# A two-block transformer on one core: the modulation vector of the second block by row products on VectorE in place of accumulated rows and one-column products on TensorE

## The reference, cut to what matters

```
cond = jax.nn.silu(c)                                   # 1 x 1024
mod = (cond @ w_ada[layer] + b_ada[layer])[:, None, :]  # 1 x 6144
sh1, sc1, g1, sh2, sc2, g2 = jnp.split(mod, 6, axis=-1)
h = rms_norm_2(x, norm1_w[layer]) * (1.0 + sc1) + sh1
...
x = x + g1 * mix
h = rms_norm_2(x, norm2_w[layer]) * (1.0 + sc2) + sh2
...
x = x + g2 * ffn
```

## Time and profile before

| | |
|---|---|
| median of 3 runs | 2187.24 us (2186.93 to 2187.7) |
| profiled execution, own time | 2188.19 us |
| its span, first to last instruction | 2186.4 us |
| TensorE busy | 2131.9 us, 98% of the span |
| VectorE, ScalarE, GpSimd busy | 1037.7, 750.0, 890.1 us |
| mean granted TensorE clock | 0.987 |

### The profile page before, as it was taken

The page is one execution under the profiler, slowest core; times in us unless marked ns, Lnnn a source line. Parts: engine busy times, 40 slices in busy tenths (PEclk is TensorE's granted clock), DMA queues, the critical chain, the costliest instruction groups (busy, mean ns, idle before and its releaser), DMA issues.

```text
span 2186.4 us, 26047 instructions
## 1 busy us (share of the span) xinstructions
PE 2131.9 (98%) x9964; PEld 1685.0 (77%) x9964; DVE 1037.7 (47%) x1726; ACT 750.0 (34%) x1106; POOL 890.1 (41%) x717
## 2 busy tenths in 40 slices
PE   7999999999999999999999989999999998999999
PEld 5888888888888445888888867767778876888887
DVE  5445653562434895566256162655655644110111
ACT  4124321222223786322122243543454333222221
POOL 4445545454433211554455334222221243454444
PEclk9999999999999999999999989999999999999999
DMA  4223333422531000342442222111111122223222
GB/s 167 96 97 135 137 118 133 171 101 73 194 115 63 1 1 20 135 153 101 156 148 101 74 92 86 41 56 58 39 58 58 57 79 77 96 77 109 103 75 99
DMA packets 34204, 204.97 MB, mean 94 GB/s; under 512 B 4160, under 2 KB 5312, under 8 KB 14784
## 3 DMA queue, kind: packets, MB, share of 16 engines
q1 hardware_dynamic: 31968, 196.84, 25.6%
q10 hardware_dynamic: 2144, 6.88, 1.0%
HBM read 199.58 MB, written 2.10 MB: 92 GB/s over the span
## 4 chain that ended last, share of the span: by engine, by line
PE 68%; issue 14%; POOL 11%; DVE 4%; ACT 1%; DMA 0%; SPq 0%; POOLq 0%; DVEq 0%; ACTq 0%
PE PS L508 14%; PE PS L509 14%; PE PS L510 14%; POOL WL L446 11%; PE PS L599 4%; PE PS L601 3%; PE PS L600 3%; PE PS L777 2%; PE PS L790 2%; PE PS L808 2%; PE PS L958 1%; PE PS L926 1%; PE PS L920 1%; PE PS L1031 1%; PE PS L899 1%
## 5 line engine op out<-in xcount | busy, mean ns | idle before, releaser
L446 POOL TENSOR_TENSOR WL<-WR,WH 128x512 fp32r<-128x512 f32 (+2 forms) x692 | 858.5, 1271 | 1186.9 <-ACT WH L1152 1186.9
L508 PE MATMUL PS<-Hh,WH 128*128 128x512 f32 x1536 | 606.2, 395 | 22.9 <-DVE Hl L1679 9.8
L509 PE MATMUL PS<-Hl,WH 128*128 128x512 f32 x1536 | 601.3, 391 | 0.0
L510 PE MATMUL PS<-Hh,WL 128*128 128x512 f32 x1536 | 600.9, 391 | 0.0
L1152 ACT ACTIVATE WH<-WR 128x2048 fp32r<-128x2048 f32 (+2 forms) x173 | 305.9, 1768 | 702.3 <-PE PS L510 661.5
L508 PEld LDWEIGHTS PS<-Hh,WH 128*128 128x128 f32 x1536 | 290.6, 189 | 89.2 <-issue 14.6
L509 PEld LDWEIGHTS PS<-Hl,WH 128*128 128x128 f32 x1536 | 290.7, 189 | 62.2 <-issue 2.2
L510 PEld LDWEIGHTS PS<-Hh,WL 128*128 128x128 f32 x1536 | 290.5, 189 | 61.0
L508 PE MATMUL PS<-Gh,WH 128*128 128x512 f32 x592 | 232.2, 392 | 0.0
L509 PE MATMUL PS<-Gl,WH 128*128 128x512 f32 x592 | 232.0, 392 | 0.0
L510 PE MATMUL PS<-Gh,WL 128*128 128x512 f32 x592 | 231.7, 391 | 0.0
(11 more groups left out here) (279 smaller groups left out, 2372.6 us busy)
## 6 DMA issues: line engine op xcount, KB each, us to landing
WR<-wA SPq DMA_DIRECT2D x125, 1024.0 KB, 4.8
AW<-wada SPq DMA_DIRECT2D x24, 1024.0 KB, 6.8
WR<-wB SPq DMA_DIRECT2D x24, 768.0 KB, 4.1
WR<-wC SPq DMA_DIRECT2D x24, 640.0 KB, 3.9
X<-x_in SPq DMA_DIRECT2D x8, 256.0 KB, 6.5
W1K<-w1k ACTq DMA_DIRECT2D x1, 2048.0 KB, 8.0
W1V<-w1v ACTq DMA_DIRECT2D x1, 2048.0 KB, 12.9
out<-X SPq DMA_DIRECT2D x8, 256.0 KB, 4.8
```

The lines of the kernel that those rows point to most:

```text
L446: ins = nc.gpsimd.tensor_tensor(WL[:, s, piece], WR[:, s, piece], WH[:, s, piece].bitcast(F32), ALU.subtract)
L508: nc.tensor.matmul(PS[:, b, :], wh[:, c, cols], pe_h, start=c == 0, stop=False)
L509: nc.tensor.matmul(PS[:, b, :], wh[:, c, cols], pe_l, start=False, stop=False)
L510: last = nc.tensor.matmul(PS[:, b, :], wl[:, c, cols], pe_h, start=False, stop=c == seg.chunks - 1)
```

## The change

`modulation_unit` no longer accumulates rows with the inputs in the partitions. `w_ada` is stored transposed, so that a unit holds 2 x 128 outputs in the partitions and all 1024 inputs of each in the free dimension. Silu(c) is needed as one row that is the same in all partitions (CROW, 128x1024). A unit is then two `tensor_tensor_reduce` instructions of 128x1024 (product with CROW into a scratch AWC, sum into one column of MOD). `mod_sums` on TensorE goes away, and the bias is added to MOD in place.

The conditioning row comes by one DMA of 512 KB from `consts`, once at the start of each of the two FFNs (unit 1 of `gu0a` and `gu1a`, ahead of that unit's `load_ada`), and ScalarE applies Silu to it after the first body of that segment (`after_first=cond_row`). The old CSIL activation and its 8 parameter columns go away.

```diff
@@ sync: segment_with_ada
                     load_unit(seg, u % seg.upb, u // seg.upb)
+                    if u == units[0] and first % 12 == 0:
+                        sp.dma_start(CROW[:, :], consts[:, C_COND:C_COND + D]).then_inc(crow_s, 16)
                     if u in units:
                         a = first + units.index(u)
                         load_ada(a, a % 2)
@@ tensor: feed_forward
-                    if r == 1:
-                        mod_sums(l)
                     down(f"dn{l}{half}", g_ready)
-            def mod_sums(l):
-                pe.wait_ge(ada_acc_s, 12 * (l + 1))
-                if l:
-                    pe.wait_ge(mod_done, 1)
-                for n in range(24):
-                    mm = nc.tensor.matmul(PS[:, 5, n:n + 1], AACC[:, n * P:n * P + P], ones[:, 0:1],
-                                          start=True, stop=True)
-                mm.then_inc(mod_sum, 1)
@@ scalar: feed_forward
+                def cond_row():
+                    act.wait_ge(crow_s, 16 * l + 16)
+                    nc.scalar.activation(CROW[:, :], CROW[:, :], ACT.Silu).then_inc(cs_s, 1)
+
-                    dense(f"gu{l}{half}", evac)
+                    dense(f"gu{l}{half}", evac, after_first=cond_row if half == "a" and l < 2 else None)
@@ scalar: start
             act.wait_ge(par_s, 16)
-            nc.scalar.activation(CSIL[:, :], pcol("cond", 0, 8), ACT.Silu).then_inc(cs_s, 1)
@@ vector: feed_forward
                     if last:
-                        dve.wait_ge(mod_sum, l + 1)
-                        nc.vector.tensor_tensor(MOD[:, 24 * l:24 * l + 24], PS[:, 5, 0:24],
+                        chain.wait()
+                        dve.wait_ge(ada_acc_s, 12 * l + 12)
+                        nc.vector.tensor_tensor(MOD[:, 24 * l:24 * l + 24], MOD[:, 24 * l:24 * l + 24],
                                                 pcol("bada", 24 * l, 24), ALU.add).then_inc(mod_done, 1)
@@ vector: modulation_unit
-                acc = AACC[:, DS(256 * f, 256)]
-                for c in range(DC):
-                    w = AW[:, slot, c * 256:c * 256 + 256]
-                    if c == 0:
-                        chain.mark(nc.vector.tensor_scalar(acc, w, CSIL[:, 0:1], None, ALU.mult))
-                        chain.wait()
-                    elif c < DC - 1:
-                        chain.mark(nc.vector.scalar_tensor_tensor(acc, w, CSIL[:, c:c + 1], acc, ALU.mult, ALU.add))
-                        chain.wait()
+                if f == 0:
+                    dve.wait_ge(cs_s, n // 12 + 1)
+                chain.wait()
+                if n:
+                    dve.wait_ge(ada_acc_s, n)
+                for b in range(2):
+                    ins = nc.vector.tensor_tensor_reduce(
+                        out=AWC[:, b, :], in0=AW[:, slot, b * D:b * D + D], in1=CROW[:, :], scale=1.0, scalar=0.0,
+                        op0=ALU.mult, op1=ALU.add, accum_out=MOD[:, 2 * n + b:2 * n + b + 1])
+                    if b:
+                        ins.then_inc(ada_acc_s, 1)
                     else:
-                        nc.vector.scalar_tensor_tensor(acc, w, CSIL[:, c:c + 1], acc, ALU.mult, ALU.add)\
-                            .then_inc(ada_acc_s, 1)
+                        chain.mark(ins)
@@ host
-        "wada": units(tiles(a["w_ada_2"][0]), 2),
+        "wada": a["w_ada_2"][0].T.reshape(24, 2, P, D).transpose(0, 2, 1, 3).reshape(24, P, 2 * D),
+    c[:, C_COND:C_COND + D] = a["c_2"][0][None, :]
```

More of the change, by code:

```diff
@@ L87 @@
           ("norm1", 8), ("norm2", 8), ("conv1", 24), ("conv2", 48), ("conv2b", 12), ("ssdn", 8),
-          ("dskip", 8), ("qn", 1), ("kn", 1), ("bada", 48), ("cond", 8), ("pek", 16), ("pev", 16),
+          ("dskip", 8), ("qn", 1), ("kn", 1), ("bada", 48), ("pek", 16), ("pev", 16),
           ("dtb", 16), ("alog", 16), ("gatew", 384), ("dtw", 128), ("w2k", 256), ("w2v", 128)]
@@ L105 @@
 C_NONES = C_NTRI + P
-C_END = C_NONES + P
+C_COND = C_NONES + P
+C_END = C_COND + D
 def tile_of(k):
@@ L191, in two_blocks @@
         EPSC = at("EPSC", 205.75, [P, 3])
-        CSIL = at("CSIL", 205.8125, [P, DC])
         MOD = at("MOD", 205.5, [P, 48])
@@ L210, in two_blocks @@
         AW = at("AW", 166, [P, 2, KMAX])
-        AACC = at("AACC", 182, [P, 24 * P])
+        CROW = at("CROW", 182, [P, D])
+        AWC = at("AWC", 186, [P, 2, D])
         KV = at("KV", 48, [P, 12, T])
@@ L309, in two_blocks @@
         ada_s = [sem("ada0_loaded"), sem("ada1_loaded")]
-        mod_sum, mod_done = sem("mod_sums"), sem("mod_done")
+        mod_done, crow_s = sem("mod_done"), sem("cond_row_loaded")
         eps_s, cs_s = sem("eps_ready"), sem("cond_ready")
@@ L1828, in _ @@
             residual("wout", next_h=(Hh, Hl, "f_norm0"))
-            dve.wait_ge(cs_s, 1)
             feed_forward(0, next_h=(Hh, Hl, "b_norm"))
@@ L2364 @@
         "qn": cols(np.concatenate([a["q_norm_w_2"][0]] * 2)), "kn": cols(np.concatenate([a["k_norm_w_2"][0]] * 2)),
-        "bada": cols(a["b_ada_2"][0]), "cond": cols(a["c_2"][0]),
+        "bada": cols(a["b_ada_2"][0]),
         "pek": cols(a["cmp_pe_k"].reshape(-1)), "pev": cols(a["cmp_pe_v"].reshape(-1)),
```

## The result

The changed kernel takes 2176.95 us (median of five runs, 2176.39 to 2178.42) beside 2187.24 us for the kernel before (median of five runs made beside it). The ratio is 0.9939 with a 95% interval of 0.9927 to 0.9951. So it is faster, as forecast, but by 10.3 us where 15.8 were forecast, and 5.5 us above the predicted 2171.5. The profiled execution took 2178.21 us, of which 2.9 lie outside its span, between 2.5 and 2.9 in all five; in the kernel before it was 1.8. So about 1 us of what is missing is not in any span, and no trace shows what it is.

A forecast was written before the change was run, and what follows sets the result against it. TensorE's own instructions were taken to bound the kernel: 2188.19 - 15.77 for the columns, all other terms 0, gave 2172.4 us, or 2171.5 since the profiled execution was 0.95 above the median; range 2167.5 to 2177.

The forecast's parts named there:

- What bounds the kernel: First FFN's modulation stretch: TensorE's own instructions are the time, 300.00 of 300.00 us busy; work taken from it is gained fully.
- The columns, 15.77 us: Between up and down segments, two places: removing one-column matmuls gains 7.07 and 8.70 us, including 4.4 us of lowered clock behind.
- Rival (a): At the two places only the columns' own 11.55 us go, the clock falls anyway: 2175.7 us, chance 0.10.
- Does a wait take the freed place? Cost 0: At the down segment's start, gate rows and first two down units' weights, needed 5 to 6 us earlier, cause no wait.
- Rival (c): Nothing moves: a new wait eats the freed place, or columns ran under another engine's cover; 2187 us, chance 0.03.
- the clock elsewhere: Clock falls outside the two places, as in attention and mixer: 2.5 us down in the forecast's own range.
- rival (d): More is gained: clock falls in attention and mixer may come out shorter, or as well longer; 2167 us, chance 0.06.
- The products, 1.22 to 1.3 us: VectorE's modulation units: each 1024-element product takes 1.22 us, 1.3 with read-out, upper bound 2.44; a unit 3.9 us.
- GpSimd beside it, 5.6 to 7.8 us: Beside a modulation unit GpSimd's four low-part pieces take 5.6 to 7.8 us, and TensorE still does not wait.
- the four tight units: In dn0a only 1.5 to 2.0 us are spare: up to 0.6 us lost per unit, 2.4 in all; taken as 0.
- Rival (b): GpSimd becomes the bound: products of 2.44 us hold it up in full, 34 us lost, 2206 us, chance 0.04.
- The conditioning row: At both FFNs' starts, the row's DMA is covered; VectorE waits 1.1 to 2.0 us for its Silu, cost 0.

The follow-up runs named there:

- e1: Kernel before with only TensorE's 48 one-column matmuls left out (bias added to columns of the accumulated rows): 2173.16 us, ratio 0.9918.
- e7: Kernel before with the one-column matmuls spread, three behind each of the eight down tiles, bias sum behind that segment: 2182.81 us, ratio 0.9960.
- e2: Changed kernel with 96 semaphore increments added to TensorE's program, 24 behind each segment of the first FFN: 2171.13 us, ratio 0.9918.
- e3: Changed kernel with ScalarE's eight row transfers per set merged into four of twice the size: 2173.13 us, ratio 0.9920.
- e4: Kernel before with 160 semaphore increments on TensorE's queue, 40 behind each segment of the first FFN: 2205.77 us, ratio 1.0067.
- e9: Changed kernel, unchanged, measured and profiled once more: 2175.25 us, ratio 0.9940.
- e10: Changed kernel with both four merged row transfers and the 96 semaphore increments on TensorE: 2175.30 us, ratio 0.9933.
- e5: Kernel of e2 with each modulation product done twice, four of 1024 elements in a unit: 2190.46 us, ratio 0.9998.
- e8: Kernel before, unchanged, measured and profiled once more: 2190.75 us, ratio 1.0007.

## Why the prediction was right, and where it was short

*What bounds the kernel.* Right. TensorE's own instructions are the time in the modulation stretch, and what was taken from it came back in full at both places.

*The columns, 15.77 us.* Right in place and size: 6.97 + 8.59 = 15.56 us measured (13.71 - 6.74 and 15.34 - 6.75). e1 shows that no other part of the change is needed for it; e7 shows the split, 4.4 us of clock, as the windows of the earlier trace rows had given. Rival (a) is out: the clock did not fall anyway.

*Does a wait take the freed place? Cost 0.* Right for the three things that it looked at, and in the profiled execution this is nevertheless the step that failed. It asked what TensorE needs at once, 5 to 6 us earlier, and closed the account there. The wait came 120 us later, at a load whose margin it never measured. In the kernel before, the last `RWK` transfer is issued at 629.64 and lands 2.3 us later, at 631.9, for matmuls that start at 632.60: 0.7 us to spare, and SyncE's weight load goes out 1.3 us behind it. One issue of 1.8 in place of 0.6 us uses up both: 1.2 and 3.8 us later, less the 0.7, is the 4.3 us of the wait. What moved was not the work against the work, which is 7.2 us earlier as a whole, but the fetch of TensorE's program against the work. Rival (c) had this shape, a new wait that eats the gain, but in the freed place and for all of it; 6.2 us of 15.6 went.

That the loss at `RWK` comes from the slow issue and the late landing is shown: e2 and e3 take it away in two unlike ways, e4 brings it into the kernel before. That the late landing comes from the large load rests on the traces alone: 6.0 to 6.2 us where the load follows within 0.2 us (after, e1, e9), 4.4 where it follows after 0.3 (e4), 2.3 where it is 1.3 to 1.4 us behind (before, e2). That the slow issue goes with the fetch rests on all ten traces with eight row transfers, in each of which one issue is slow (1.31 to 1.84 us) and a packet of queue 8 starts within 0.15 us of its start, and on two kernels where padding TensorE's program moved both. The traces with four transfers (e3, e10) say nothing on it. How the one delays the other is not shown.

*The median.* 2171.5 less 1.8 is a span of 2169.7 us; the median execution has 2174.1, so 4.4 of the 5.5 us lie in the span and 1.1 outside it. Its clock of 0.989 is that of the executions with the fall in the second mixer. With the wait for `RWK` on top its span would be about 2168.5 + 6.2 + 5.9 = 2180.6 (the span of e2, the loss at `RWK`, and what e10 has over e2), and no execution of the changed kernel was that long. So the wait is the miss of the profiled execution and of one like it, and for the median, as far as spans and clocks tell, the term that failed is the one for the clock elsewhere: the forecast's own range has 2.5 us down for it and nothing up, and only a half-sentence of rival (d) says that it may come out longer. Why the clock falls there in some executions stays open, and so does the 1.1 us.

*The products, 1.22 to 1.3 us.* Right where one runs alone: 1.22 us and 0.08 for the read-out. Beside GpSimd it is up to 2.31. The timeline of VectorE, ScalarE and GpSimd after, in a unit without modulation work and the one behind it with two products:

```profile
229.99 5.04 POOL L449 TENSOR_TENSOR WL<-WR,WH 128x512 fp32r<-128x512 f32 x4 [3.82 <-ACT WH L1143]
...
240.72 1.22 DVE L1803 CUSTOM_DVE_ANT_0 AWC<-AW,CROW 128x1024 f32<-128x1024 f32 x1
240.87 7.40 POOL L449 TENSOR_TENSOR WL<-WR,WH 128x512 fp32r<-128x512 f32 x4 [5.84 <-ACT WH L1143]
...
241.87 2.31 DVE L1803 CUSTOM_DVE_ANT_0 AWC<-AW,CROW 128x1024 f32<-128x1024 f32 x1
```

The unit takes 3.5 us (244.18 - 240.72; forecast 3.9), and VectorE's busy time of 953.7 us lies in the 930 to 980.

*GpSimd beside it, 5.6 to 7.8 us.* Right: 7.40, which is 2.36 more than 5.04 and just twice 1.18. That each product holds GpSimd for its full length was the upper bound of the sum, not what it took, and it is what the trace fits: GpSimd loses twice nearly a product's 1.22 us, and the second product lasts 1.09 us longer than the first, less than one GpSimd piece (5.04 / 4). The Trainium skill says so (SBUF — State Buffer, section "SBUF: two separate sides": the shared ports are held as a lock for the whole instruction); the trace agrees with it, and more closely than with my reason for taking 0, that the first product starts before GpSimd does. It cost nothing since GpSimd ends at 248.27 and TensorE wants the low part at about 249.8: 1.5 us are spare where 3.2 were before. In `dn0a` GpSimd's pieces lasted 4.96 us (4.71 in the earlier trace rows), and the 2.4 us kept for the four tight units were not needed. Rival (b) is real as a mechanism and stayed 1.5 us short of the first wait: e5 meets it at four products.

*The conditioning row.* Right. VectorE waits for its Silu 1.13 us twice (1.1 to 2.0 expected), with nothing behind it. The start is worth 0, with the same 5.2 us of wait for GpSimd.

*More is gained (d).* In part: the second mixer came out 1.6 us shorter in the profiled execution, and the swing seen in e7, e8 and e10 is a clock fall in just such a place. It goes the other way and by more than the rival allowed, and it isn't tied to the change.

The forecast fits the kernel of e2, where no wait is added: 2171.13 us measured, 2171.5 predicted. That this is within 0.4 us is in part luck: e2 also has the 1.6 us of the second mixer, which the sum didn't count, and its four executions spread over 4.9 us. In the range given, 2167.5 to 2177.0, the result of 2176.95 stands at the upper edge, for reasons that the range was not made from; that it lies inside is luck.

## What to carry to other kernels

When work is taken from the bounding engine, follow one instruction that both kernels have through the whole run: the gain and what is given back later then stand apart, and the second is the place to work on. But a profile explains its own execution only: set span and mean clock of the others beside it before the median is put down to what it shows. A load whose margin is a microsecond or two deserves fewer and larger DMAs before it is hurt, since here a change in the length of a program far ahead took such a margin away. And the block of one-column matmuls cost more than its own time, by the clock behind it (4.4 us for 11.5); where such a block can't be moved to another engine, a few behind each dense tile are the next best, as e7 shows.

## What the runs showed of the hardware that I had not expected

- In each of the ten traces with eight row transfers one issue on ScalarE's queue took 1.31 to 1.84 us where the others took 0.62, and a 16 KB packet that goes with TensorE's program started within 0.15 us of its start. With four transfers of twice the size the fourth took 1.10 to 1.18 us each time, with such a packet near or not.
- A 120 KB transfer issued 0.15 us ahead of a 1 MB load landed after 6.1 us, and after 2.3 where the load came 1.3 us behind.
- Increments of a semaphore in TensorE's program cost nothing in four blocks of 24, and 14.3 us in four blocks of 40, part of it by a lower clock (0.77 from 500 to 530).
- The granted clock in the second mixer from 1480 to 1550 differs between executions of one kernel (1.00 or 0.82 in the same 20 us), worth 3 to 5 us. What decides it stays open; so does the number of unprofiled executions in which the changed kernel had the wait for `RWK` (it stands in both profiles of it and in that of e1, and spans and clocks speak for one of the other four measured with the first).
